# Value and z_attn projections with two weight panels side by side: 512 columns a matmul, four heads a group

## The reference, cut to what matters

```
h = RMSNorm(x)
q, k, v, z_a, u_glu, z_c, ga, gc = split(h @ w_in)      # v, z_a, z_c: 1024 columns each
# branch A: 8 heads, two softmax maps each, value width 128 a head
a = softmax(q1 k1) - lam * softmax(q2 k2)                # causal
o = RMSNorm_per_head(a @ v) * (1 - lam_init)
y_attn = (o * silu(z_a)) @ w_o_attn
# branch B
u = layer_norm(causal_depthwise_conv(glu(u_glu)))
y_conv = (silu(u) * silu(z_c)) @ w_pw2 + b_pw2
# merge
m = sigmoid(ga) * y_attn + sigmoid(gc) * y_conv
out = x + RMSNorm(m @ w_out)
```

## Time and profile before

| | |
|---|---|
| time, median of 3 runs | 1209.65 us (1208.23 to 1210.04) |
| profiled execution | 1209.35 us, span of its slowest core 1207.8 us |
| even cores (0, 2, 4, 6), span | 1205.1 to 1207.8 us |
| odd cores (1, 3, 5, 7), span | 1196.9 to 1202.4 us |
| busy on core 4 | TensorE 1100.8 us (91%), VectorE 580.2 (48%), ScalarE 298.8 (25%), GpSimd 102.0 (8%) |
| stages on core 4 | z_attn with three convolutions from 200.2 us; first values 404.5 to 420.3; attention 420.3 to 687.7 |

### The profile page before, as it was taken

One profiled execution on the slowest core, in us unless ns is written; L12 is line 12 of the kernel. 1 busy time (PEld: TensorE's weight loads), 2 busy tenths in 40 slices (PEclk: granted clock), 3 DMA queues, 4 the chain that ended last, 5 costly groups with the idle time before them and its releaser, 6 DMA issues.

```text
span 1207.8 us, 21800 instructions; the slowest of 8 cores (1196.9 to 1207.8 us)
## 1 busy us (share of the span) xinstructions
PE 1100.8 (91%) x8030; PEld 674.5 (56%) x8042; DVE 580.2 (48%) x1377; ACT 298.8 (25%) x442; POOL 102.0 (8%) x196
## 2 busy tenths in 40 slices
PE   2697999999999997798777899999999999999995
PEld 1354556886666764466444556666666666654442
DVE  5572453426644267767777743333333333314433
ACT  3441133431111243344434321111111111102111
POOL 2010101110211100000000001011011010000000
PEclk9898999999999998899899989999999999999998
DMA  8937857643755532202232215063473482263442
GB/s 255 212 46 158 145 117 140 116 73 73 143 106 103 129 57 54 55 15 62 56 71 36 36 35 105 2 105 55 86 140 60 81 133 42 37 175 139 157 161 102
DMA packets 49359, 116.93 MB, mean 97 GB/s; under 512 B 5472, under 2 KB 11872, under 8 KB 45920
## 3 DMA queue, kind: packets, MB, share of 16 engines
q0 software_dynamic: 27648, 62.93, 32.2%
q1 hardware_dynamic: 21312, 52.35, 14.2%
q10 hardware_dynamic: 288, 0.18, 0.0%
HBM read 161.76 MB, written 16.58 MB: 148 GB/s over the span
## 4 chain that ended last, share of the span: by engine, by line
PE 78%; DVE 12%; issue 4%; ACT 3%; DMA 2%; DVEq 1%; SPq 0%; ACTq 0%
PE ps L1271 20%; PE ps L815 10%; PE ps L1323 10%; PE ps L769 9%; PE ps L648 9%; PE ps L1281 5%; PE ps L1275 5%; PE ps L692 3%; PE ps L921 2%; PE ps L1018 2%; DVE zoz L967 1%; DVE r L955 1%; PE ps L898 1%; DMA r<-usc 1%; DVE r L944 1%
## 5 line engine op out<-in xcount | busy, mean ns | idle before, releaser
L1271 PE MATMUL ps<-hTo,wring 128*128 128x384 bf16 x1536 | 258.2, 327 | 0.0
L1271 PEld LDWEIGHTS ps<-hTo,wring 128*128 128x128 bf16 x1536 | 150.6, 98 | 99.9 <-issue 1.0
L164 POOL DMA_DIRECT2D wring<-wp x176 | 93.4, 547 | 862.5 <-PE ps L1271 243.9
L648 PE MATMUL ps<-hTo,wring 128*128 128x384 bf16 x768 | 131.9, 334 | 9.9 <-ACT hTo L544 4.2
L769 PE MATMUL ps<-wring,hTo 128*128 128x256 bf16 x1152 | 137.1, 274 | 1.2 <-PE ps L898 1.2
L1288 ACT ACTIVATE zoz<-zoz 128x384 f32<-128x384 f32 x96 | 50.0, 522 | 317.3 <-DVE zoz L1286 317.3
L815 PE MATMUL ps<-hTo,wring 128*128 128x384 bf16 x768 | 125.0, 326 | 0.0
L769 PEld LDWEIGHTS ps<-wring,hTo 128*128 128x128 bf16 x1152 | 109.4, 98 | 21.8 <-issue 8.1
L904 ACT ACTIVATE r<-ps 128x1024 bf16<-128x1024 f32 (+2 forms) x104 | 93.2, 905 | 94.1 <-PE ps L898 72.4
L1286 DVE TENSOR_TENSOR zoz<-ps,R 128x384 f32<-128x384 f32 x96 | 53.5, 558 | 129.7 <-PE ps L1271 129.7
L648 PEld LDWEIGHTS ps<-hTo,wring 128*128 128x128 bf16 x768 | 75.9, 100 | 64.0 <-issue 17.9
(11 more groups left out here) (115 smaller groups left out, 1044.1 us busy)
## 6 DMA issues: line engine op xcount, KB each, us to landing
wring<-wp POOLq DMA_DIRECT2D x176, 256.0 KB, 7.2
r<-usc SPq DMA_DIRECT2D x32, 295.2 KB, 5.9
hTo<-xr SPq DMA_DIRECT2D x9, 1024.0 KB, 6.4
out<-hTo SPq DMA_DIRECT2D x18, 512.0 KB, 3.3
r<-xf SPq DMA_DIRECT2D x11, 768.0 KB, 9.0
r<-wop POOLq DMA_DIRECT2D x4, 1024.0 KB, 13.8
zoz<-wop POOLq DMA_DIRECT2D x4, 1024.0 KB, 15.0
r<-wout POOLq DMA_DIRECT2D x4, 1024.0 KB, 20.7
```

Source lines behind the costliest of these rows:

```text
L164: eng.dma_start(out=it[1][0], in_=it[1][1]).then_inc(self.dsem[it[2]], 16)
L648: t.op('pe', lambda e, dc=dc, x=x: e.matmul(bank(2 * par + x, n), lhsT=w[:, dc, 128 * x:128 * x + 128], rhs=hTo[:, dc, c:c + n], start=(dc ...
L1271: t.op('pe', lambda e, dc=dc, k=k, w=w, o=o, cs=cs, c0=c0, n=n: e.matmul(o[k], lhsT=w[:, dc, cs], rhs=hTo[:, dc, HALO + c0:HALO + c0 + n], ...
```

## The change

z_attn, the values and their panels are taken two panels at a time. The panels of the values are put next to each other in the ring (z_conv's four come behind them), `panel2` views two slots as one moving operand of 2 x 256 columns, and a unit is one tile of 128 tokens with 16 matmuls of 512 columns (four heads) that fill a bank, in four pieces of 4. `VA` has two buffers of four heads. So the values of heads 0 to 3 are made ahead of the attention and those of heads 4 to 7 are filler: on an even core all in quarter 0, on an odd one in quarters 0 and 1. z_conv's chunks go to quarters 1 to 3 (2, 2 and 4; on an odd core 3 and 5 in quarters 2 and 3). The copies out of PSUM take 512 columns an instruction. The places of the three convolutions among z_attn's units follow.

```diff
-    p += [rng(C_V), rng(C_V + 256), rng(C_ZC), rng(C_V + 512), rng(C_V + 768), rng(C_ZC + 256), rng(C_ZC + 512), rng(C_ZC + 768)]
+    p += [rng(C_V + 256 * g) for g in range(4)] + [rng(C_ZC + 256 * g) for g in range(4)]
...
-P_V = (20, 21, 23, 24)
-P_ZC = (22, 25, 26, 27)
-LAST = {0: 2, 1: 2, 2: 3, 12: 15, 13: 15}
+P_V = (20, 22)
+P_ZC = (24, 25, 26, 27)
+LAST = {0: 2, 1: 2, 2: 3, 12: 15, 13: 15, 8: 11, 10: 13, 20: 23, 22: 25}
...
-    VA = [m.bf(NK * 260).rearrange("p (m h e) -> p m h e", m=NK, h=2) for k in range(2)]
+    VA = [m.bf(NK * 520).rearrange("p (m h e) -> p m h e", m=NK, h=4) for k in range(2)]
...
+    def panel2(k):
+
+        load_upto(LAST[k])
+        slot = k % 4
+        v = wring[:, 4096 * slot:4096 * (slot + 2)].rearrange("p (s a n) -> p a s n", s=2, a=16)
+        return v, [[('W', slot, c), ('W', slot + 1, c)] for c in range(4)]
+
+    def proj_chunks(pk, kt, banks, evac):
...
-            for dc in range(8 * (c % 2), 8 * (c % 2) + 8):
-                t.op('pe', lambda e, dc=dc: e.matmul(bank(b, 256, 256 * x), lhsT=get(dc), rhs=w[:, dc, :], start=(dc == 0), stop=(dc == 15)),
-                     reads=[box['rw'][dc // 4]] + rd, writes=[('ps', b)], sig=(dc == 15 and x == len(tiles) - 1))
-            if c == 2 * len(tiles) - 1:
+            get, rd = tok_tile(kt)
+            for dc in range(4 * c, 4 * c + 4):
+                t.op('pe', lambda e, dc=dc: e.matmul(bank(b).rearrange("p (s n) -> p s n", s=2), lhsT=get(dc), rhs=w[:, dc, :, :],
+                                                     start=(dc == 0), stop=(dc == 15)),
+                     reads=box['rw'][dc // 4] + rd, writes=[('ps', b)], sig=(dc == 15))
+            if c == 3:
...
-    zu = [(g, u) for g in range(4) for u in own_units]
+    zu = [(g, u) for g in range(2) for u in range(NX // 128, NK)]
     for n, (g, u) in enumerate(zu):
-        if n in (3, 8, 13):
+        if n in (2, 6, 10):
             next_conv()
...
-    for u in units(0, NK):
-        for f in v_unit(0, u, kb):
+    for kt in range(NK):
+        for f in v_unit(0, kt, kb):
             f()
...
-        zcu = [(cc, k) for cc in ((0,), (1,), (2,), (3, 4, 5, 6, 7))[g] for k in range(NG)]
-        if g == 1:
-            for cc, k in zcu:
-                fill += zc_pieces(cc, k, fb)
-        if g < 3:
-            for u in units(0, NK):
-                fill += v_unit(g + 1, u, fb)
-        else:
+        chunks = ((), (0, 1), (2, 3), (4, 5, 6, 7))[g] if half == 0 else ((), (), (0, 1, 2), (3, 4, 5, 6, 7))[g]
+        zcu = [(cc, k) for cc in chunks for k in range(NG)]
+        tiles = (range(NK), (), (), ()) if half == 0 else (range(8), range(8, 16), (), ())
+        for kt in tiles[g]:
+            fill += v_unit(1, kt, fb)
```

More of the change, by code:

```diff
@@ L867, in program, with v_unit @@
     vcnt = [0]
[L869 to L870 removed]
+    def v_unit(g, kt, banks):
         def evac(b):
             vcnt[0] += 1
[L874 to L880, removed]
[L881 to L884 removed]
+            sv = bank(b).rearrange("p (h e) -> p h e", h=4)
+            dv = VA[g][:, kt, :, 0:128]
+            rc = rcol[:, kt:kt + 1]
+            if vcnt[0] % 2:
+                t.op('act', lambda e: e.activation(out=dv, in_=sv, func=AF.Copy, scale=rc), reads=[('ps', b), 'rcolo', 'rcolx'], writes=[('VA', g, kt)])
+            else:
+                t.op('dve', lambda e: e.tensor_scalar(out=dv, in0=sv, scalar1=rc, scalar2=None, op0=ALU.mult),
+                     reads=[('ps', b), 'rcolo', 'rcolx'], writes=[('VA', g, kt)])
+        return proj_chunks(P_V[g], kt, banks, evac)
     pairs = [(h,) + st for h in range(8) for st in H.steps()]
@@ L913, in emit_pv @@
         h, si, q0, nq, ent, first, last = pairs[n]
-        slot, hl = (h // 2) % 2, h % 2
+        slot, hl = h // 4, h % 4
         et = ET[n % 3]
@@ L1144, in program @@
     zb = Banks([0, 1, 2, 3])
-    own_units = units(NX // 128, NK)
-    zu = [(g, u) for g in range(4) for u in own_units]
+    zu = [(g, u) for g in range(2) for u in range(NX // 128, NK)]
     for n, (g, u) in enumerate(zu):
-        if n in (3, 8, 13):
+        if n in (2, 6, 10):
             next_conv()
-        if NX and n == 14:
+        if NX and n == 12:
             oth_factors()
-        if NX and n == 15:
+        if NX and n == 13:
             oth_spread()
@@ L1194, in program @@
         fill = []
-        zcu = [(cc, k) for cc in ((0,), (1,), (2,), (3, 4, 5, 6, 7))[g] for k in range(NG)]
-        if g == 1:
-            for cc, k in zcu:
-                fill += zc_pieces(cc, k, fb)
-        if g < 3:
-            for u in units(0, NK):
-                fill += v_unit(g + 1, u, fb)
-        else:
-            t.handover(oth_res + lnbuf + ['cw', ('lj', 0), ('lj', 1)], ozT_all + [('wop', 0)] + ([('wop', 1)] if NX else []))
[L1204 to L1210, removed]
-                        fill.append(turns.pop(0))
-            assert g < 3 or not turns
+        chunks = ((), (0, 1), (2, 3), (4, 5, 6, 7))[g] if half == 0 else ((), (), (0, 1, 2), (3, 4, 5, 6, 7))[g]
[3 more added lines that the diff above has]
+            fill += v_unit(1, kt, fb)
+        if g == 3:
+            t.handover(oth_res + lnbuf + ['cw', ('lj', 0), ('lj', 1)], ozT_all + [('wop', 0)] + ([('wop', 1)] if NX else []))
+        turns = [f for h in range(6) for f in oz_turns(h, fb)]
+        for n, (cc, k) in enumerate(zcu):
+            fill += zc_pieces(cc, k, fb)
+            if g == 3 and n >= 2:
+                left = len(zcu) - n
+                for _ in range(-(-len(turns) // left)):
+                    fill.append(turns.pop(0))
+        assert g < 3 or not turns
         weights = [1.0 for pr in pairs[per * g:per * g + per] for y in range(2 if pr[6] else 1)]
```

29 lines of the change are left out of this document (10 added, 19 removed).

## The result

The changed kernel takes 1224.40 us (median; 1223.12 in the profiled execution) against 1209.65 before. The ratio, made from the executions of 1223.12 and 1224.40, is 1.0116, 95% interval [1.0099, 1.0134]: the kernel is 1.2% slower. The time lies in the predicted range of 1211 to 1229, and 6.5 us above the predicted 1217.9. Executions in which cores of a die were disturbed are left out of every ratio and of the medians of the experiments, and where a profile has such a die (runs e4, e7 and e9), cores of the other die are read.

A forecast was written before the change was run, and what follows sets the result against it. The even cores set the time, with VectorE's work bounding the attention from head 1 on. Values +15.3, z_attn -1.1 and attention -5.7 gave +8.5 on 1209.35, so 1217.9 us, range 1211 to 1229.

The forecast's parts named there:

- The sign: Whole kernel: slower by over 0.2%, given a chance of 0.86.
- the cause: Even cores: VectorE's work sets the attention from head 1 on, so it gives back only 5.7 us against +15.3.
- The first value stage: Even cores, ahead of the attention: 144 matmuls go from 256 to 512 columns, 15.8 to 31.1 us, +15.3, copies hidden.
- The width: All paired matmuls: 3.9 ns saved a pair, 2.2 us in all 576, of which z_attn's part is -1.1.
- the third rival: Value and z_attn matmuls: 256 columns lose far more than their pitch shows, pairs gain some 20 us, 1198 us; 2%.
- Heads 1 to 5: Attention, even cores: changes of -3.3, -3.2, +2.9, +3.7 and -0.5 us, head by head.
- Head 2's wait for exps: Attention, head 2: VectorE's 3.2 us of waiting goes with the 40 value matmuls behind it, -3.2; 0 if it stays.
- Heads 6 and 7: three units less, -7.8: Last quarter of the attention: three z_conv units fewer, at 2.6 us of VectorE each, shorten both heads together by 7.8 us.
- Head 0: First head of the attention: 19.6 value pieces instead of 16.4, TensorE the bound, +2.5 us.
- The slow clock as a rival: Four z_conv heads in a row fall to TensorE's slow clock, 3.2 us each, +12.8, 1231 us; 22%.
- The wash: Attention gives back all 16.4 us of filler taken from TensorE, 1207.2 us, not slower; 11%.
- The odd cores: First value stage +27.2 us, partly given back: 1212 at the worst from 1202.4, below the even cores' 1216.

The follow-up runs named there:

- e4: Kernel before, with VectorE's work behind z_conv's tanh moved to GpSimd (three instructions for two, second tanh buffer): 1238.66 us, ratio 1.0219.
- e7: Kernel after, with 288 surplus matmuls of 128 columns among z_conv's pieces in quarters 1 and 2 of the even cores: 1225.68 us, one execution, no ratio.
- e9: Kernel after, with one batch of transposes behind each z_conv unit of the last quarter, even cores only: 1223.1 us, ratio 1.0108.
- e1: Kernel before, with z_attn alone taken two panels at a time: 1209.90 and 1211.25 us, against 1209.90 to 1212.99 before.
- e2: Kernel after, with each matmul of 512 columns split into two of 256, same order: 1224.43 us, ratio 1.0113.
- e5: Kernel after, with the copy of a slot's sums out of PSUM moved from VectorE to ScalarE: 1207.26 us, ratio 0.9977.
- e6: Kernel before, with the copy of a slot's sums out of PSUM moved from VectorE to ScalarE: 1189.3 us, ratio 0.9827.
- e10: Kernel before, with two batches of transposes behind the third and fourth z_conv units of the last quarter, even cores only: 1212.9 us, ratio 1.0023.
- e8: Kernel after, even cores: later values over quarters 0 and 1, z_conv units 3, 6, 6 and 9 a quarter: 1226.70 us, ratio 1.0147.

## Why the prediction came out as it did

The sign, the cause and the range held; the sum came out 5.3 us short on core 4's span (13.8 measured, 8.5 forecast). The misses are +1.05 in the value stage, +0.3 from it to the first PV, +1.4 in head 0 and +4.4 in heads 6 and 7. Some 0.9 us less ahead of the values and 1.0 less behind the attention, which nothing forecast, made the sum look better than its terms.

**The first value stage: right, 1 us short.** +15.3 was forecast, +16.35 measured. The matmuls took 31.24 us (31.1); the rest is the 0.93 us that QK waits for the last copy, which I called hidden. It is hidden behind the next matmuls of each unit but the last.

**The width: right.** z_attn gained 0.7 us with the pairs (e1), and the first value stage is 0.4 us longer without them (e2); the totals of e1 and e2 show no more, and the third rival, which needed some 20 us, is out.

**Heads 1 to 5: right.** Forecast 28.2, 32.8, 30.4, 31.9 and 31.0 us, measured 27.3, 31.7, 31.4, 31.2 and 32.7: 154.3 and 154.3 in sum. The equal sums are luck: single heads are off by 0.7 to 1.7 us either way. VectorE still fills heads 2 to 5: head 3 is 23.93 us of work, 2.3 of waits for the tanh, 0.4 for an exp, and 92 x 0.052 between instructions, 31.4. Head 2's wait for exps went, as forecast. e5 and e6 show the bound by taking work off VectorE, e7 by adding work to TensorE.

**"Heads 6 and 7: three units less, -7.8" is the step that failed, as a term taken too large.** Together they went from 82.9 to 79.5 on core 4, -3.4 (-3.4 on core 6 too, -5.4 on cores 0 and 2). Head 7 gave 3.8. In head 6 VectorE's work fell by 2.3 us (32.98 to 30.69), and the tanh waits from 6.2 to 4.7, which makes the 3.8 us that half of the three units should free; but VectorE then waited 3.2 us for z_conv's matmuls, 0.8 for PV and 0.5 within its own queue. The runs put some 2 us of this on the transposes in pairs (e9, e10) and 1.2 to 1.9 on the slow clock (sister cores of e9 and of the kernel after). That the number of units sets where the transposes go stands in the code; I hadn't followed it.

**Head 0: 1.4 us over** (29.6 forecast, 31.00 measured). Core 2 runs the same program:

```profile
439.10:468.80 29.70, 28.48 (x229) 14.27 (x228) 16.68 (x60) 12.97 (x16) 1.12 (x3) 1.00 0.47 85
```

There it takes 29.70 at full clock, against 31.00 at 0.95, and TensorE is busy for 28.48 instead of 29.79 us with the same 229 matmuls: the excess is the slow clock's, and TensorE bounds this head. It stood for 0.93 and 0.89 us just ahead of the head on both cores, so what made the clock fall on one of them alone isn't shown. At full clock the forecast held.

**The slow clock as a rival** was put in the wrong place. The time of 1224.4 lies where that rival's band began, but of heads 2 to 5, which it named, only head 2 shows a price: 31.7 us at 0.89 on core 4 (VectorE waits 0.6 us for PV there), 30.9 at 0.94 on core 2. Its larger prices stand in head 0 (1.3 us) and head 6 (1.9), and not on every even core: core 4 pays all three, core 2 none. Since the slowest core counts, the kernel pays for whichever has it.

**The wash** is refuted: 16.4 us less filler were worth nothing in the heads of core 4, and at most 2.9 us on another. **The odd cores** stayed below, at 1210.3 us at most (1212 at the worst was forecast).

Open: up to 1 us of head 6 and the 1.7 us that head 5 ran over (1.0 of it two waits of VectorE for an exp); and why heads 6 and 7 gave e8 so little, where other waits than the pairs' (for exps and for z_conv at a slow clock) took VectorE's time.

## What to carry to other kernels

Work that fills the idle slots of an engine that isn't the bound is almost free there, as long as the slots hold it (e7); moved ahead into a stage where that engine is full, it costs its whole length, so a wider instruction must pay for its schedule as well as for itself. Before taking such work out, find the engine whose busy time, overheads and waits add up to the stage, and move that engine's work instead: here one copy moved from VectorE to ScalarE was worth 20 us, 1.7%. And when the number of pieces changes, look at everything that is dealt out by that number.

## What was not expected of the hardware

VectorE's masks and scalings on SBUF operands didn't run beside GpSimd's work: 22 masks of e4's core 0 that overlapped z_conv's work on GpSimd took up to 1.03 us, the other 50 at most 0.29, while the reads of PSUM that overlapped it (L944 twice, L1025 once) and three reciprocals of 4 elements (L945) took no longer than alone. And the same program had another granted clock in the same head on sister cores of one execution: 0.95 and 1.00 in head 0, 0.87 and 0.90 in head 6.
